# A two-block transformer layer on one core: the experts' phase as a loop on TensorE and SyncE, with another order of loads

## The reference, cut to what matters

```python
def moe_ffn(h, w_router, b_router, w1, b1, w2, b2):
    logits = (hf @ w_router + b_router).astype(jnp.float32)
    top_val, top_idx = lax.top_k(logits, TOP_K)          # 4 of 32 experts a token
    ...
    def expert_block(args):
        xb, e = args
        hh = xb @ w1[e] + b1[e]                          # 1024 -> 2048
        return swiglu_clamped(hh) @ w2[e] + b2[e]        # 1024 -> 1024
    ...
    out = jnp.einsum('tk,tkd->td', gates.astype(y.dtype), y)
```

## Time and profile before

| What | Value |
|---|---|
| Median of 3 runs | 1447.84 us (1447.49 to 1448.01) |
| The profiled execution | 1447.14 us; its span 1445.4 us |
| Busy, share of the span | PE 1310.7 us (91%), PEld 792.7, DVE 533.5 (37%), ACT 398.5 (28%) |
| Chain that ended last | PE 63%, DMA 22%, DVE 6%, ACT 4%, issue 3% |
| Matmuls of the up pieces, L1306 | 3392, in 53 passes |
| Matmuls of the down pieces, L1325 | 3392, in 53 passes |
| Loads of expert weights, issued | 36 of 4 MB, 119 of 2 MB, 2 of 1 MB |
| Granted TensorE clock, mean | 0.98 of full speed |

### The profile page before, as it was taken

One profiled execution on the slowest core, in us unless ns is written; L12 is line 12 of the kernel. 1 busy time (PEld: TensorE's weight loads), 2 busy tenths in 40 slices (PEclk: granted clock), 3 DMA queues, 4 the chain that ended last, 5 costly groups with the idle time before them and its releaser, 6 DMA issues.

```text
span 1445.4 us, 32784 instructions
## 1 busy us (share of the span) xinstructions
PE 1310.7 (91%) x13192; PEld 792.7 (55%) x13192; DVE 533.5 (37%) x1082; ACT 398.5 (28%) x742; POOL 0.2 (0%) x4
## 2 busy tenths in 40 slices
PE   9999999999999998999999899786997879978896
PEld 8998679998688663343444344232443334433343
DVE  6833677885597762212121122111221212111122
ACT  6734445553455641111111111010110101111112
POOL 0000000000000000000000000000000000000000
PEclk9999999999999999999999999999999999999999
DMA  9431985455773599999999999999999999999995
GB/s 366 176 118 59 397 337 197 189 193 194 269 316 114 219 394 432 426 426 428 427 428 427 426 429 431 433 426 427 436 425 427 432 428 428 433 426 429 435 423 245
DMA packets 31342, 508.46 MB, mean 352 GB/s; under 512 B 3504, under 2 KB 3632, under 8 KB 4912
## 3 DMA queue, kind: packets, MB, share of 16 engines
q1 hardware_dynamic: 31248, 507.08, 83.9%
HBM read 506.02 MB, written 1.05 MB: 351 GB/s over the span
## 4 chain that ended last, share of the span: by engine, by line
PE 63%; DMA 22%; DVE 6%; ACT 4%; issue 3%; SPq 0%; DVEq 0%; ACTq 0%
PE acc L1306 21%; DMA low<-in_w 15%; PE acc L535 9%; PE acc L1325 8%; DMA high_part<-in_w 5%; PE acc L1296 3%; PE acc L1264 3%; PE acc L998 2%; PE acc L573 2%; DMA low<-in_stream 2%; PE acc L1271 1%; PE acc L574 1%; DVE w_lo L1506 1%; ACT high_part L1925 1%; PE acc L1346 1%
## 5 line engine op out<-in xcount | busy, mean ns | idle before, releaser
L1306 PE MATMUL acc<-low,high_part 128*32 128x512 f32 x2384 | 290.3, 617 | 51.0 <-DMA low<-in_w 38.6
L2519 DVE TENSOR_SCALAR high_part<-acc 128x256 f32<-128x256 f32 x53 | 22.5, 424 | 505.9 <-PE acc L1306 505.9
L1306 PEld LDWEIGHTS acc<-low,high_part 128*32 128x32 f32 x2384 | 86.8, 113 | 212.5 <-issue 160.6
L1325 PE MATMUL acc<-low,high_part 128*32 128x256 f32 x2624 | 152.6, 383 | 8.2 <-DMA low<-in_w 8.2
L1923 ACT ACTIVATE high_part<-high_part 128x256 f32<-128x256 f32 x53 | 22.1, 417 | 470.5 <-DVE high_part L2519 470.5
L1506 DVE TENSOR_TENSOR w_lo<-low,w_hi 128x4096 fp32r<-128x4096 f32 (+1 forms) x30 | 130.5, 4352 | 35.7 <-ACT w_hi L1500 35.3
L1306 PE MATMUL acc<-high_part 128*32 128x512 f32 x1008 | 121.3, 608 | 12.5 <-DMA high_part<-in_w 9.1
L1325 PEld LDWEIGHTS acc<-low,high_part 128*32 128x32 f32 x2624 | 82.4, 110 | 71.9 <-issue 18.2
L1500 ACT ACTIVATE w_hi<-low 128x4096 fp32r<-128x4096 f32 (+1 forms) x28 | 99.8, 3569 | 56.4 <-DMA low<-in_stream 50.7
L1296 PE MATMUL acc<-high_part 32*128 32x256 f32 x864 | 77.1, 425 | 14.9 <-ACT high_part L1940 11.6
L535 PE MATMUL acc<-x_hi,w_hi 128*128 128x256 f32 x352 | 85.5, 284 | 0.8 <-DVE x_lo L1534 0.7
(11 more groups left out here) (499 smaller groups left out, 1803.0 us busy)
## 6 DMA issues: line engine op xcount, KB each, us to landing
low<-in_w SPq DMA_DIRECT2D x36, 4096.0 KB, 36.2
low<-in_w SPq DMA_DIRECT2D x68, 2048.0 KB, 28.6
high_part<-in_w SPq DMA_DIRECT2D x51, 2048.0 KB, 33.4
low<-in_stream SPq DMA_DIRECT2D x41, 2048.0 KB, 8.1
high_part<-in_stream SPq DMA_DIRECT2D x4, 2048.0 KB, 12.1
high_part<-in_natb SPq DMA_DIRECT2D x1, 2048.0 KB, 13.5
low<-in_w SPq DMA_DIRECT2D x2, 1024.0 KB, 41.3
high_part<-in_rows SPq DMA_DIRECT2D x1, 1536.0 KB, 14.1
```

The lines of the kernel that those rows point to most:

```text
L1306: last = mm(flat[32 * q:32 * q + 32, 2048:2560], XG[:, b, 32 * kk:32 * kk + 32], wp[:, 2048 * b + 512 * q:2048 * b + 512 * q + 512], start ...
L1325: last = mm(flat[32 * q:32 * q + 32, 2816:3072], AT[:, 128 * (c % 2) + 32 * (c // 2):128 * (c % 2) + 32 * (c // 2) + 32], wp[:, 1024 * (c ...
L2519: ts(GLU, flat[:, 2048:2304], 7.0, None, ALU.min).then_inc(S("glu"), 1)
```

## The change

TensorE's and SyncE's code for the experts becomes a loop of 15 rounds, two experts a round, with experts 0, 1 and 31 (and the last loads) outside. For that, slots are fixed: up pieces of an even turn in slots 0 to 3, of an odd one in 4 to 7; the first down piece in slot 10 (even) or 8 (odd); the second down piece, of every turn, in slot 9. All loads are of 2 MB, but for the last piece in two halves, as before. The second down piece of expert j is issued between the second and third up piece of expert j + 2, and waits for the downs of expert j - 1, the last use of slot 9. The first loads, which come before the loop, go to the same slots at the same signals, but bring other pieces: expert 0's first down piece early, its second one and expert 1's first last.

```diff
@@ -48,21 +48,14 @@
-EXPERT_PIECES = [(0, r) for r in range(6)] + [(1, r) for r in range(5)]
-for _j in range(2, NE):
-    EXPERT_PIECES += [(_j, r) for r in range(4)] + [(_j - 1, r) for r in ((5,) if _j == 2 else (4, 5))]
...
-DOUBLE = {_n for _n, (_j, _r) in enumerate(EXPERT_PIECES) if _r % 2 == 0 and EXPERT_PIECES[_n + 1] == (_j, _r + 1)
-          and _n % NSLOT < NLOW - 1 and 6 * NSLOT + 6 <= _n < 6 * NE - 4}
...
+NAHEAD = 2
+def expert_slot(odd, r):
+    return 4 * odd + r if r < 4 else 9 if r == 5 else (10, 8)[odd]
@@ SyncE
-            for n in range(NSLOT, 6 * NE):
-                if n - 1 in DOUBLE:
-                    continue
-                j, r = EXPERT_PIECES[n + 1 - NSLOT if n in DOUBLE else n - NSLOT]
...
-                released(last, r)
-                if n in DOUBLE:
-                    expert_pieces(e, n)
-                else:
-                    expert_piece(e, n)
+            def up_pieces(j, odd, between=None):
+                last, e = last_pass(j - NAHEAD), expert_in_turn(j)
+                for r in range(3):
+                    if r == 2 and between:
+                        between()
                     sp.wait_ge(S("wused"), 3 * last + r + 1)
+                    expert_piece(e, odd, r)
+                sp.wait_ge(S("w1"), last + 1)
+                expert_piece(e, odd, 3)
+            def down_piece_4(j, odd):
+                last, e = last_pass(j - NAHEAD), expert_in_turn(j)
+                sp.wait_ge(S("w2_half"), last + 1)
+                expert_piece(e, odd, 4)
+            def down_piece_5(j, odd):
+                last, e = last_pass(j - 1), expert_in_turn(j)
+                sp.wait_ge(S("w2"), last + 1)
+                expert_piece(e, odd, 5)
+            up_pieces(2, 0)
+            down_piece_5(1, 1)
+            down_piece_4(2, 0)
+            up_pieces(3, 1)
+            with sp.Fori(1, NE // 2 - 1) as i:
+                up_pieces(2 * i + 2, 0, lambda: down_piece_5(2 * i, 0))
+                down_piece_4(2 * i + 1, 1)
+                up_pieces(2 * i + 3, 1, lambda: down_piece_5(2 * i + 1, 1))
+                down_piece_4(2 * i + 2, 0)
+            down_piece_5(NE - 2, 0)
+            down_piece_4(NE - 1, 1)
+            last, e = last_pass(NE - 2), expert_in_turn(NE - 1)
+            sp.wait_ge(S("w2"), last + 1)
+            last_piece(e)
@@ TensorE
-            for j in range(2, NE):
-                next_first, next_turns = passes_of(j)
-                ups(j, next_first, next_turns)
-                downs(j - 1, first, turns, next_first + next_turns)
-                first, turns = next_first, next_turns
-            downs(NE - 1, first, turns, first + turns)
+            with pe.Fori(0, NE // 2 - 1) as i:
+                first, turns = passes_of(2 * i + 2)
+                ups(i + 1, 0, first, turns)
+                downs(i, 1, *passes_of(2 * i + 1), first + turns)
+                next_first, next_turns = passes_of(2 * i + 3)
+                ups(i + 1, 1, next_first, next_turns)
+                downs(i + 1, 0, first, turns, next_first + next_turns)
+            first, turns = passes_of(NE - 1)
+            downs(NE // 2 - 1, 1, first, turns, first + turns, last_half)
```

More of the change, by code:

```diff
@@ L387, in _, with expert_piece @@
             sp.wait_ge(S("ada"), SIDE[-1] + 1)
-            sp.dma_start(slot_of(NSLOT - 1), w2[1:2, :, 0:NPIECE].rearrange("a p n -> (a p) n")).then_inc(S(f"slot{NSLOT - 1}_loaded"), 16)
+            sp.dma_start(slot_of(NSLOT - 1), w2[0:1, :, 0:NPIECE].rearrange("a p n -> (a p) n")).then_inc(S(f"slot{NSLOT - 1}_loaded"), 16)
             for piece_ in (("in2", 5), ("out", 1)):
                 load(N_OF[piece_])
[L392 to L400, removed]
+            def expert_piece(e, odd, r):
+                s = expert_slot(odd, r)
@@ L413, in _, with last_piece @@
+            def last_piece(e):
+                s = expert_slot(1, 5)
+                for signal, c in ((f"slot{s}_loaded", 0), ("last_half", NPIECE // 2)):
+                    sp.dma_start(slot_of(s)[:, c:c + NPIECE // 2],
+                                 w2[bass.ds(1 * e, 1), :, NPIECE + c:NPIECE + c + NPIECE // 2].rearrange("a p n -> (a p) n"))\
+                      .then_inc(S(signal), 16)
             sp.wait_ge(*used(N_OF["in2", 5]))
-            expert_piece(0, 2)
-            expert_piece(1, 7)
+            expert_piece(0, 0, 2)
@@ L437, in last_pass @@
             def last_pass(j):
-                return sp.value_load(passes[0:1, 72 + NE + j:73 + NE + j], min_val=0, max_val=NPMAX - 1)
-            def released(last, r):
-                if r < 3:
-                    sp.wait_ge(S("wused"), 3 * last + r + 1)
-                else:
-                    sp.wait_ge(S(("w1", "w2_half", "w2")[r - 3]), last + 1)
-            of_last, of_expert = None, None
-            for n in range(NSLOT, 6 * NE):
-                if n - 1 in DOUBLE:
-                    continue
-                j, r = EXPERT_PIECES[n + 1 - NSLOT if n in DOUBLE else n - NSLOT]
[L453 to L457, removed]
-                released(last, r)
-                if n in DOUBLE:
-                    expert_pieces(e, n)
-                else:
-                    expert_piece(e, n)
+                return sp.value_load(passes[0:1, bass.ds(j + 72 + NE, 1)], min_val=0, max_val=NPMAX - 1)
@@ L1383, in _, with loader, ups @@
             pe.wait_ge(*step("cum_in"))
-            def loader(j):
+            def loader(half_j, odd):
                 def loaded(r):
[L1388 to L1391, removed]
+                    s = expert_slot(odd, r)
+                    loads = half_j + 1 if r < 5 else 2 * half_j + odd + 1
+                    pe.wait_ge(S(f"slot{s}_loaded"), 16 * loads + 16 * slot_base[s])
+                    return slot_of(s)
                 return loaded
             def passes_of(j):
-                return (pe.value_load(passes[0:1, j:j + 1], min_val=0, max_val=NPMAX - 1),
-                        pe.value_load(passes[0:1, j + NE:j + NE + 1], min_val=1, max_val=MAXPASS))
-            def ups(j, first, turns):
+                return (pe.value_load(passes[0:1, bass.ds(j, 1)], min_val=0, max_val=NPMAX - 1),
+                        pe.value_load(passes[0:1, bass.ds(j + NE, 1)], min_val=1, max_val=MAXPASS))
+            def ups(half_j, odd, first, turns):
                 with pe.Fori(0, turns) as r:
-                    up_pass(first + r, loader(j))
+                    up_pass(first + r, loader(half_j, odd))
             def last_half():
@@ L1408, in last_half, with downs @@
                 pe.wait_ge(S("last_half"), 16)
[L1410 removed]
+            def downs(half_j, odd, first, turns, made, half=None):
                 with pe.Fori(0, turns) as r:
[L1413 removed]
+                    down_pass(first + r, made, loader(half_j, odd), half)
             first, turns = passes_of(0)
[L1416 removed]
+            ups(0, 0, first, turns)
             gates()
[L1418 to L1426 removed]
+            downs(0, 0, first, turns, first + turns)
+            ups(0, 1, *passes_of(1))
+            with pe.Fori(0, NE // 2 - 1) as i:
[7 more added lines that the diff above has]
+            downs(NE // 2 - 1, 1, first, turns, first + turns, last_half)
             n_passes = pe.value_load(passes[0:1, 64:65], min_val=NE, max_val=NPMAX - 1)
```

42 lines of the change are left out of this document (11 added, 31 removed).

## The result

| What | Value |
|---|---|
| Median of 4 runs | 1473.11 us (1472.25 to 1477.35); before 1447.92 (1447.49 to 1448.17, 4 runs) |
| Ratio | 1.018, 95% interval 1.016 to 1.020: slower, by just under 2% |
| The profiled execution | 1472.25 us; its span 1470.3 us |
| Forecast | 1464 us, range 1455 to 1473 |

Slower, as forecast, in the places forecast, but by 25 us and not by 16; the median lies 0.1 us outside the range. First the page: its engines, the slices of 37 us, the queues.

The account below looks back on a forecast made before the run. Loading the experts' weights, 192 pieces of 2 MB on full DMA engines, was taken to set the end. Terms: 12 dry, some 9 at the end, 3 for doubles, 8 back from code: 16 us slower, 1464 us, range 1455 to 1473.

Parts of the forecast that it names:

- dry, three stretches: Load queue empty near 680, 694 and 727 us, around experts 5 to 7: 4.1, 3.0 and 5.0 us, 12 in all.
- the reload: TensorE reads two pass numbers before odd experts' downs: 1.5 us each, between 0 and 3.1.
- The upper bound, 3.1: Highest price considered for one pass-number read before odd downs, from a pass behind such a gap taking 9.0 instead of 7.3 us.
- each reload drops the clock: Rival: each pass-number read before odd downs costs 3.1 us, giving 1468 us; chance 0.12.
- Register work: Other register work on TensorE at a turn of the loop: 0.1 us.
- wait at expert 3: TensorE waits 2.0 us for expert 3's late fourth up piece, plus some 0.8 for the slower start behind it.
- The first stretch: Near 680 us, the queue is dry for 4.1 us until expert 7's first up piece, which needs expert 5's last pass.
- Doubles, +3: Splitting 36 loads of 4 MB into loads of 2 MB costs 3 us, between 0 and 4.
- Code, -8: TensorE's loop stops instruction fetches, removing five load pauses of 1.6 us after 690 us: -8 us, or 0 if it fetches.
- Some 9 at the end where one load stands alone: The last piece, sharing slot 9, is issued only after expert 30's downs and lands alone: some 9 us.
- empty stretches in the middle: Named as a sign of error: that 44 us of released loads do not cover a heavy expert.
- The sign: Whole kernel slower, chance 0.92; faster 0.06, within 0.2% of no change 0.02.

Follow-up runs that it names:

- e10: The changed kernel with two idle matmuls of 384 columns on TensorE ahead of the two pass-number reads before odd experts' downs; 1467.18 us.
- e5: The kernel before, with every 4 MB load split into two of 2 MB in the same slots and order; 1450.23 us.
- e2: The changed kernel with TensorE's 15 rounds written out instead of looped; reads, slots and SyncE's loop stay; 1472.44 us.
- e1: The changed kernel with an odd expert's two pass numbers read behind the even expert's up matmuls, not between last up pass and downs; 1464.53 us.
- e3: The changed kernel with TensorE's rounds written out and odd experts' pass numbers kept in registers instead of read again; 1467.20 us.
- e6: The changed kernel with the very last piece in free slot 0, issued ahead of expert 30's second and expert 31's first down piece; 1470.46 us.
- e7: The changed kernel with the edits of e1 and e6 together; 1461.54 us.
- e8: As e7, but SyncE's loads written out in another order, each piece no earlier than its slot comes free; same slots; 1454.09 us.
- e4: The changed kernel with the loop's second down piece issued one place later, between third and fourth up piece; 1476.01 us.
- e11: The changed kernel plus some 645 instructions at the end of TensorE's program, in a loop with turn count 0; 1601.60 us.

## Why the prediction was wrong in size and right in place

| Station | Forecast | Measured | Late by |
|---|---|---|---|
| queue first empty | 679.3 | 681.6 | 2.3 |
| dry, three stretches | 4.1 + 3.0 + 5.0 = 12.1 | 6.6 + 3.2 + 7.2 = 17.0 | 4.9 more |
| expert 27's second down piece lands | 1352.6 | 1359.5 | 6.9 |
| expert 29's second up pass | 1373.4 | 1379.5 | 6.1 |
| downs of expert 30 end | 1442.2 | 1450.7 | 8.5 |
| last landing | 1449.7 | 1458.1 | 8.4 |
| end of the span | 1462.0 | 1470.3 | 8.3 |

The step that failed is the reload: "I take 1.5, the length of the row itself, and 0.1 for other register work at a turn." Each part was too small. The upper bound, 3.1, was the truth: in the idle time of 1.6 us the clock falls (with the gap filled, in e10, it doesn't), and the work behind it pays as much again. The rival "each reload drops the clock", with a chance of 0.12, is what happened; it gave 1468. The reads of experts 1, 3, 5 and 29, 1.6 us dearer each, make some 6.4 of the 8.3 us at the end. Register work was 0.3 to 0.8 us a turn and 0.1 a pass, most of the rest. Expert 5's last pass came 10.8 us later than before instead of 6.1: 3.2 and 3.1 for the reads before downs 1 and 3, 2.8 of wait at expert 3 (as forecast), 1.9 for turns and passes, less 0.25 from the passes ahead. The first stretch was to be 4.1; with the 4.7 by which this pass came later than forecast, and less the 2.3 by which the queue was emptied later, it is 6.5. Expert 5's own read and the turn ahead of it lengthen the third. At the end, expert 29's read and the turns add 2.4 once more.

The 2.3 at the first station were in no term: the experts' first load is issued at 483.58 instead of 481.00 us, in the same code as before. All kernels with the whole loop start at 482.6 to 483.6 us, all four written out at 481.0 to 481.5. That the end doesn't show them is luck. The queue runs dry and waits for TensorE: the landing behind the first dry stretch, 693.05 against a forecast of 688.3, is as late as expert 5's last pass. And TensorE, which begins expert 0's ups 2.7 us later than before, makes it good, since the up passes of experts 0 and 2 took 9.0 us before and take 7.3 here: it ends expert 2's ups at 573.81 instead of 574.05 us, which is the 0.25 above.

The other terms. Doubles, +3: 2.7 (e5). Code, -8: the pauses did go (e2 has them, 9.6 us), but the loop's own cost, the late start and dearer turns, took them back: net nothing with the reads in the open, 2.7 by the medians and 4.9 by the spans with them hidden (e1 against e3). The wait at expert 3: 2.8, as forecast. "Some 9 at the end where one load stands alone" read the end wrongly: the sum itself followed TensorE there, rightly, and the load costs TensorE a wait of 0.76 us and a last pass that is 1.0 us longer (e6).

Of what the new profile should show: few packets of code, yes; dry near 680, 694 and 727 us and after 1425, full between, yes; waits in downs of experts 15, 21 and 27 of 7.7, 7.2 and 8.2 us, yes, and of expert 9 only 2.5; the last piece issued some 7 us before its landing, yes, but at 1450.9. What was named as wrong, empty stretches in the middle, did not come.

The sign was never close. Order and single loads alone cost 19.5 us (e3), and 2.7 of that is the loads' size. With reads hidden and the last piece moved, the loop in this order still is 14 us behind (e7), of which another order in the same slots gives back 7.4 (e8).

## What to carry to other kernels

Price a gap on TensorE at both ends: the idle time itself, and the work behind it at half the clock; if the gap can't go, filling it with idle matmuls took some 4 to 6 us off here. In a load list, a piece that waits for a late event holds up every free slot behind it: place it by when its slot comes free and when it is needed, in the turn that is worst (e8 against e7, 7.4 us). A loop that saves code loading has costs per turn and may shift other parts; take the saving and these costs as separate terms. And when a run meets the expected time, look in its trace for the expected working: e4 and e6 met the first and, at best in part, the second.

## What the hardware showed that had not been expected

The clock doesn't always fall behind the same gap, and no run shows what decides it. In the changed kernel TensorE idled for some 1.6 us ahead of all 15 odd downs, and stayed at full clock in three (experts 15, 19 and 25; expert 19's pass took 3.66 us). Ahead of expert 2's ups, 4.0 to 4.1 us lie between the matmuls of two passes in all looped kernels, and the pass behind took 7.3 us in the changed kernel and 9.0 in e4 and e8. With 0.32 us of idle time (e10) it fell behind no read.

A loop whose turn count is 0 by the code ran once (e11). And lone loads of 2 MB from the same tensor, in code that no edit touched, took 8.3 to 8.5 us in kernels whose TensorE program has the loop, 8.0 with half of it and 7.5 to 7.6 without; the cause is open.
